# PEER block with the last projection units moved into the second half of their stages

## What is computed

```
hn = rmsnorm(x);  proj = hn @ w_in              # conv channels, gates, a few head columns
x  = x + concat(ssd(...), gated_delta(...)) @ w_out     # causal, in tiles of 128 tokens
h  = rmsnorm(x);  scores = (h @ w_q) against 2 x 128 keys, 8 heads -> top 16 of 256 pairs
idx, gates = 128 experts per token (8 heads x 16), softmax
act = gelu(sum_d h[t,d] * u_tab[idx[t,k],d])            # U: 128 rows of 4 KB per token
x  = x + sum_k gates*act * v_tab[idx[t,k],:]            # V: 128 rows of 4 KB per token
out = rmsnorm(x)
```

## Time and profile before

| | us |
|---|---|
| median of 3 runs | 3428.85 (3428.53, 3428.85, 3438.62) |
| the profiled execution: its own time | 3437.05 |
| its span, from first to last instruction | 3435.3 |
| PE, DVE, ACT, POOL busy | 2539.3, 2073.3, 561.3, 1975.4 |
| first gather of stages 1, 2, 3, 4 | 728.6, 1125.7, 1516.2, 1903.8 |
| first gather of stages 5, 6 | 2241.5, 2581.9 |

### The profile page before, as it was taken

How to read it: one execution, slowest core, us unless ns; L and a number is a source line. 1 busy time by engine, 2 the same in 40 slices (tenths; PEclk the granted TensorE clock), 3 DMA queues, 4 the chain that set the end, 5 groups by cost and what they waited for, 6 DMA issues and landing times.

```text
span 3435.3 us, 27404 instructions
## 1 busy us (share of the span) xinstructions
PE 2539.3 (74%) x9080; PEld 1040.8 (30%) x9080; DVE 2073.3 (60%) x4704; ACT 561.3 (16%) x1160; POOL 1975.4 (58%) x2097
## 2 busy tenths in 40 slices
PE   6876389847887678867888577857885878566698
PEld 5763265414331243213431142113211421111121
DVE  3343676887575666766575677667766776544300
ACT  3341144412121212112110110011001100000000
POOL 1100233345566556666666677767776777777775
PEclk8988699969999899998999899989998999898999
DMA  5530477889999999999999999999999999999998
GB/s 153 195 133 1 167 245 263 295 323 349 339 385 364 377 334 382 388 393 360 367 381 356 407 394 409 407 408 388 409 409 407 400 409 408 409 409 409 409 404 354
DMA packets 356957, 1185.38 MB, mean 345 GB/s; under 512 B 41984, under 2 KB 73104, under 8 KB 356560
## 3 DMA queue, kind: packets, MB, share of 16 engines
q0 software_dynamic: 297072, 1079.97, 81.2%
q1 hardware_dynamic: 58592, 99.47, 8.5%
q10 hardware_dynamic: 1152, 4.19, 0.3%
HBM read 1159.82 MB, written 23.66 MB: 345 GB/s over the span
## 4 chain that ended last, share of the span: by engine, by line
POOL 24%; DMA 24%; PE 22%; DVE 13%; issue 10%; ACT 2%; SPq 0%; DVEq 0%; ACTq 0%; POOLq 0%
POOL ring L869 24%; DMA ring<-in_peer_v_dram,picks_T 14%; DMA ring<-in_peer_u_dram,picks 9%; PE y_psum L946 7%; DVE ring L1319 4%; PE b_bank L901 3%; PE y_psum L901 2%; PE tile_psum L1099 2%; PE tile_psum L1078 2%; DVE arena L1552 1%; DVE arena L1556 1%; PE tile_psum L1040 1%; DVE arena L1559 1%; PE tile_psum L1041 1%; PE tile_psum L1022 1%
## 5 line engine op out<-in xcount | busy, mean ns | idle before, releaser
L946 PE MATMUL y_psum<-ring,spread 128*32 128x512 f32 x4096 | 1359.9, 648 | 517.5 <-DMA ring<-in_peer_v_dram,picks_T 516.3
L1319 DVE CUSTOM_DVE_ANT_0 ring<-ring,h_psum 128x1024 f32<-128x1024 f32 x1024 | 1236.3, 1218 | 809.2 <-DMA ring<-in_peer_u_dram,picks 795.1
L869 POOL DMA_INDIRECT ring<-in_peer_u_dram,picks x1024 | 972.7, 950 | 864.9 <-DVE dots L1319 267.9
L869 POOL DMA_INDIRECT ring<-in_peer_v_dram,picks_T x1024 | 969.5, 947 | 431.5 <-issue 261.2
L946 PEld LDWEIGHTS y_psum<-ring,spread 128*32 128x32 f32 x4096 | 263.4, 114 | 1501.5 <-DMA ring<-in_peer_v_dram,picks_T 890.1
L1099 PE MATMUL tile_psum<-w_q,arena 128*128 128x512 f32 x512 | 224.9, 597 | 1.1 <-ACT arena L1275 1.1
L1178 ACT COPY spread<-zero 128x8 f32<-128x8 f32 (+1 forms) x104 | 21.6, 208 | 861.2 <-PE y_psum L946 861.1
L901 PE MATMUL b_bank<-ring 128*128 128x384 f32 (+1 forms) x464 | 156.0, 490 | 0.0
L1099 PEld LDWEIGHTS tile_psum<-w_q,arena 128*128 128x128 f32 x512 | 97.0, 191 | 122.8 <-issue 119.4
L1078 PE MATMUL tile_psum<-w_out,arena 128*128 128x512 f32 x256 | 120.9, 617 | 1.1 <-ACT arena L1262 1.1
L1347 DVE SCALAR_TENSOR_TENSOR res<-res,stat_e,final_row 128x1024 f32<-128x1024 f32 x8 | 10.3, 1283 | 176.7 <-ACT stat_e L1195 176.7
(11 more groups left out here) (242 smaller groups left out, 2351.0 us busy)
## 6 DMA issues: line engine op xcount, KB each, us to landing
ring<-in_w_units_dram SPq DMA_DIRECT2D x42, 512.0 KB, 6.4
ring<-in_peer_u_dram,picks POOLq DMA_INDIRECT x1024, 7.8
ring<-in_peer_v_dram,picks_T POOLq DMA_INDIRECT x1024, 8.5
w_blk<-in_w_units_dram SPq DMA_DIRECT2D x28, 512.0 KB, 4.0
ring<-in_w_q_T_dram SPq DMA_DIRECT2D x16, 512.0 KB, 3.5
res<-in_w_units_dram SPq DMA_DIRECT2D x14, 512.0 KB, 5.7
arena<-tok_scr SPq DMA_DIRECT2D x8, 768.0 KB, 9.2
arena<-zgs_scr SPq DMA_DIRECT2D x8, 520.0 KB, 21.8
```

Of the source, the lines that this page charges most:

```text
L869: pool.indirect_dma_start(ring[:, j], None, tables[kind], bass.IndirectOffsetOnAxis(ap=at, axis=0)).then_inc(filled[j], 16)
L946: last = nc.tensor.matmul(y_ps[quad * STEPS:(quad + 1) * STEPS, half], lines[:, quad, at:at + STEPS], ring[:, j, half * BANK:(half + 1) * ...
L1319: nc.vector.tensor_tensor_reduce(out=ring[:, j], in0=ring[:, j], in1=h_ps[:], scale=1.0, scalar=0.0, op0=ALU.mult, op1=ALU.add, accum_out= ...
```

## The change

One line of `with_units`. `begin` is the gather of the list behind which the first unit of a stage stands, and `gap` the number of gathers from B to K and from K to D. The units of a stage are spread evenly from `begin` to the end of the stage's list of 248 gathers (the last 8 V come behind it).

```diff
-    begin, gap = (1, 2) if e == 0 else (16, 5)
+    begin, gap = (1, 2) if e == 0 else (128, 3)
     points = []
     for n in range(first, to):
         at = begin + (total - begin - 3 * gap) * (n - first) // (to - first)
         points += [(at, n, "BQ"), (at + gap, n, "KZ"), (at + 2 * gap + (e == 0), n, "DY")]
```

## The result

The changed kernel takes 3450.38 us (median of 8 runs, 3442.86 to 3460.67), the kernel before 3428.69 us (median of 8, 3426.39 to 3439.22). The ratio is 1.0055, 95% interval 1.0038 to 1.0072: 19 us slower (21.7 by the medians). The forecast was 3443 us, 14 us slower. The profiled execution took 3449.02 us, its span is 3447.2 us, 11.9 longer than before. That it is less than 19 goes with the execution profiled before, which was a long one, 8.4 us above the median of its kernel.

The account below looks back on a forecast made before the run. POOL's issue and the DMA transfers, at 1.24 us a gather, were taken as the floor. The terms, 44 + 21 - 51 = +14 us, on the median of 3428.85 us gave 3443 us, range 3408 to 3470.

Parts of the forecast that it names:

- The bound and the mechanism of a stand: Gather ring: floor of 1.24 us a gather; a 5.43 us block on PE fills seven slots, so POOL stands 4.46 us.
- Two smaller signs: Profile after: POOL's waits for PE fall to 15 to 20 us in first halves, reach 50 and more in second.
- The smaller gap: From block to D, 6 gathers: PE may wait at D, costed at nothing; without cover some 3 us a unit.
- Leaving the first halves: Stages 1 to 3, before gather 124: five units leave each, saving 51 us, bounds 39 and 77.
- Unit 47's stand: V stretch: POOL stands 4.46 us behind its block, 4.2 more than usual, taken as a unit's price.
- Arriving: Second halves, stages 1 to 3: nine more units in the V stretch cost 44 us, six in the U stretch 21.
- the rival of no change: Both halves: a unit costs its block wherever it stands, what leaves one half arrives in the other; 3429 us, chance 0.22.
- The third rival: Moved units: a unit's own chain bounds, +59 us (3488) or +36 (3465), POOL standing longer than 7 us; chance 0.15.
- The free places: Where only U are read, DVE reads the slots: one block is free in the U stretch, a third doesn't fit.

Follow-up runs that it names:

- the base: Changed kernel with all 29 third-part units in stage 1 (begin 16, gap 3), none in stages 2 and 3: 3466.95 us, ratio 1.0103 to the kernel before.
- The runs on the places: Changed kernel with gap 5 and `begin` 64, ratio 0.9987, or `begin` 96, ratio 1.0001, both to the kernel before.
- The two attempts: Kernel before, gap 5, with blocks at gathers 1 and 14 (3439.96 us, ratio 1.0022), or with three blocks in the U stretch (ratio 1.0031).

## Why the forecast held, and what in it was wrong

The size and the sign were right, 14 us of some 19, the halves nearly: 189 us was measured where 187 was forecast, 207 where 210 was. The account behind them was wrong in one step and off in three, and that the sum came out is in part luck.

**The bound and the mechanism of a stand** held. POOL's pace is the floor. Behind the 17 blocks from gather 177 on (172 in stages 2 and 3), POOL's longest wait for PE is 2.2 to 6.5 us, above 4 at 14 of them. Stages 0 and 4 to 8 are as they were. Two smaller signs missed: 20.9 to 26.5 us of waits for PE are left in the first halves, not 15 to 20, and the second halves have 44.8 to 49.1, not 50 and more.

**"The smaller gap" is the step that failed.** I costed it at nothing, with the ring just emptied as the cover. The gap alone, at the old places, costs 0.51%, as much as the change (0.55%). The cover wasn't whole: behind the wait of 1.75 us above, the next matmuls of V found their gathers landed. What of the gap costs is D near the block (1.0081 alone) and not K near it (1.0008). By which path it costs is open. PE's wait for SiLU at D is there, but it is 9.5 us in the run with the gap alone, which lost some 17, and stage 3 is 13.1 us longer than before in that run with none of it, and 8.6 in the changed kernel with 1.8. Nor is the gap's share in the changed kernel known by itself, since at its places a gap of 5 is worse and D at 8 is no better.

**"Leaving the first halves"** was given 51 us and measured 39.2, its lower bound, and less if stage 1 is taken from a shorter execution. Seven slots alone account for 13 us of a half's surplus, which I had taken for a third of it, 7 to 9 us in stages 2 and 3. Unit 47's stand, 4.2 us, was too dear a model as well: the net price there is 2.2 us a unit, 2.7 if the one at gather 16 is free.

**"Arriving"** was given 65 us and measured 53.4. The same windows, cut again at gather 176, part the two stretches: gathers 128 to 175 of the three stages took 207.7 us before and 215.6 now, gathers 176 to 255 took 359.7 and 405.2. The stands of the two blocks at 172, 4.6 and 6.4 us, lie behind the cut. So the U stretch took about 8 us without them, where I had 21 with them, and the third block there was cheap; PE was 44.03 of 48.1 us busy in it, not throughout. A stand of POOL isn't the price of a block: it takes in shorter waits that seven slots would bring anyway (a second half without units has 17 to 20 us of them), and a block's net price in the second half is 2.7 us, and 3.2 in the changed kernel. Both terms were too large by the same 12 us, so that the difference came out: luck.

**How the loss divides.** With room the place costs nothing that can be told (0.9987 and 1.0001). By the base, a stage 2 or 3 of the changed kernel is 7.7 us longer than before (396.7 against 389.05): ten units at the second half's old price of 2.7 against five at 2.2 and five at 2.7 would be 2.5, and the rise from 2.7 to 3.2 is 5 more. That rise is no more than gap 3 brings at the old distance (3.4). The runs on the places can't tell 2.5 us a stage from none. So the rival of no change was right on the places. The third rival, a unit's own chain, is the nearest to what the runs show of the gap, though at a fraction of its price, and POOL's stands stayed below its 7 us. Unexpected for it: the gap of 5, which is better at the old places, is much worse at 11 gathers from block to block (1.0130), where D is followed at once by the next block, which waits for the copy. The changed kernel's gap of 3 is the lesser evil at a distance that allows neither.

**The free places.** The two attempts to use places taken for free brought no gain. At the start of the stage the next wait is for what SP issues, the weights and the store; for the U stretch the one trace leaves it open.

## What to carry to other kernels

A chain that passes through several engines (block, taps, SiLU, transposes, copy, store) and has one buffer needs distance between its links and to the next chain; when units are put closer, cost both distances, since one can be bought only from the other. A wait that shows up with a loss isn't yet its cause: see whether it lies in the stages that lost. Ask whether the execution profiled is near the median of its kernel. Before splitting a stretch's surplus between two causes, run one kernel that has only one of them. A stand in the timeline isn't its net price: compare stretches with and without it.

## What was not expected of the hardware

The seven-slot ring costs its 13 us a first half in many short waits, none for PE above 2.8 us, although seven gathers at 1.24 us are 8.7 us and a gather lands in 6.0 us. And chips differ. Where the kernel with `begin` 96 ran, the second half of a stage like stage 5, without units and with eleven slots, takes 188.3 us against 163.6, with the DMA engines' share at 0.96. That window, and the rate over it in 40 slices:

```profile
2538.60:2726.90 188.30, 135.20 (x381) 34.62 (x380) 120.43 (x338) 10.98 (x26) 120.43 (x129) 0.91 0.96 361
...
GB/s 364 410 412 412 409 287 326 293 381 418 411 408 410 407 410 408 123 325 384 406 212 333 406 401 271 330 419 411 340 333 298 324 362 266 307 410 413 413 407 358
```

In the kernel before, all slices of the same stretch lie between 404 and 414. So the transfers don't run slower throughout on that chip: they keep about 410 GB/s for half of the slices and fall in between, to as little as 123. No run shows why.
